# Expert picks of 64 tokens at a time: 64-column weight matrices in the two column halves of the array, in a one-core hybrid decoder step

## The chip, the core and the metric

One NeuronCore of one Trainium2 chip runs the whole program. The metric is device time in microseconds (us), as the median of several runs; durations inside the program come from one profiled execution. TensorE (PE in the profile) multiplies, VectorE (DVE), ScalarE (ACT) and GpSimd (POOL) do elementwise work, SyncE (SP) issues plain transfers, and sixteen DMA engines move data between HBM and SBUF. PEld in the profile is TensorE's weight load, which runs beside the multiplications.

## The reference

The program computes one step of a small decoder layer for 512 new tokens of one sequence and for 8 sample tokens of running sequences: two kinds of attention, an output projection, and then a layer of product-key experts ("PEER"). The change lies in the experts:

```
def peer(h, wq, subkeys, pu, pv):          # h: tokens x 1024
    q = (xb @ wq).reshape(blk, 8, 2, 128)
    s = einsum('thpc,hpnc->thpn', q, subkeys)          # 8 heads, 2 halves, 128 keys
    sv, si = top_k(s, 16)
    cand = sv[:, :, 0, :, None] + sv[:, :, 1, None, :]
    fv, fi = top_k(cand, 16)                            # 16 experts per token and head
    eidx = the expert numbers (of 16384);  gate = softmax(fv)
    act = gelu(einsum('thkd,td->thk', pu[eidx], xb)) * gate
    return einsum('thk,thkd->td', act, pv[eidx])
```

Each token has 8 heads of 16 picks. For each pick a row of `pu` (1024 floats) is multiplied with the token's row and summed, and a row of `pv` (1024 floats) is added to the token's result with the weight that comes of it. The two rows of an expert lie side by side in one table `peer_uv`, so a pick is one row of 8 KB. All data are float32.

## The kernel before

Before the experts come the projections, the attention and the page reads of the sample tokens; they take the first 870 us or so and none of that part is touched. The experts of the 512 prompt tokens are worked off in 4 tiles of 128 tokens, each of 8 heads, so in 32 units of 16 picks. A **step** is one pick of one head for all 128 tokens of a tile: there are 512 of them, and 8 more, one for each sample token with all its 128 picks, put in after unit 27. Steps are numbered g in the order in which they run.

For each step:

- `gather` on POOL issues one indirect DMA that brings 128 rows of 8 KB (1 MB), one for each partition, into one of `UN` = 8 buffers `UV` (six in the big ring `RING`, two in `R1` and `R2`). It first waits until `v_used` says that PE has finished step g - 8, the one before it in that buffer. On the same queue of POOL nothing else happens in this part.
- `dot` on DVE multiplies the first half of each row with the token's row `H2` and sums it (`SCALAR_TENSOR_TENSOR`, line 1797).
- `gelu` on ACT (line 1114) and `weigh` on DVE (line 1815) turn the sums of two steps into weights. They work on pairs of steps, so the second step of a pair holds back both.
- `diagonal` on ACT (line 1124) writes a matrix `DG` of 128 x 128: the identity, with each row scaled by its token's weight. There are 4 of them in turn.
- `value_step` on PE multiplies `DG` with the second half of the gathered rows, 512 columns at a time, and adds it in two PSUM banks (`lo`, `hi`) that a tile keeps for all its 128 steps:

```
pe.wait_ge(S(f"uv_in{g % UN}"), 16 * (g // UN + 1))
pe.wait_ge(S("diagonal"), k + 1)
mm(lo[:, :], DG[:, k % 4, :], UV[g % UN][:, 1024:1536], first, last)
mm(hi[:, :], DG[:, k % 4, :], UV[g % UN][:, 1536:2048], first, last, S("v_used"))
```

The order on every engine is written out by hand along **events** e: at event e POOL issues the gather of step e + 3, DVE takes the dot of step e, ACT at odd e the gelu of the steps e - 1 and e and the diagonals of e - 3 and e - 2, PE the value step of e - 4.

Between the steps of one tile the preparation of the next one is threaded in as **slots**, one at an event: 8 slots `wo` (`mix_part`: the output projection of the tile, two multiplications of 512 columns each; tile 3 has 16 of them, half of them for the 8 sample tokens), some for a norm and its transposes ("rest", "turn"), and 40 for queries and scores (`wq`, `score`). DVE works off the picks of the unit after next in pieces between its dots (`picks`), ACT the softmax of the gates (`gates`, with a table load before and one after it), DVE their scaling (`gate_scale`). At the start of each tile DVE takes the sums of the tile before out of PSUM, adds the residual, and normalises it. After the last step the last tile's sums go the same way. SP loads the weights of the slots (2 MB at a time), the tokens' rows and small vectors, and stores the results.

Of the kernel before, what the change touches and what calls it, by code (L numbers as in the profile page):

```python
# [8 lines left out]
ALU = mybir.AluOpType  # L9
# [3 lines left out]
P = 128  # L13
# [5 lines left out]
TILES = SEQ // P  # L19
# [13 lines left out]
def hybrid_decoder_step(nc, a, o):  # L33

    ctx = ExitStack()
    with ctx:
# [115 lines left out]
        G1S = part(R1, 7296, 1024)  # L152
        X1 = part(R1, 8320, 2048, n=2, d=D_MODEL)
# [7 lines left out]
        G2, G2S, FW = MV[:, 0, :], MV[:, 1, :], MV[:, 2, :]  # L161
# [26 lines left out]
        DG = part(R2, 11628, 512, n=4, c=P)  # L188
# [221 lines left out]
        def _(pe):  # L410
# [455 lines left out]
            def value_step(g, n, s_):  # L866
                t, h = divmod(n, PH)
                k = n * STEPS + s_
                lo, hi = banks[(t % 2) * 2], banks[(t % 2) * 2 + 1]
                first, last = h == 0 and s_ == 0, h == PH - 1 and s_ == STEPS - 1  # L870
# [17 lines left out]
            for e in events:  # L888
# [4 lines left out]
                elif n is not None:  # L893
                    value_step(g, n, s_)
# [10 lines left out]
        def _(act):  # L905
# [174 lines left out]

            def query_out(i, c, j):
# [34 lines left out]
            def diagonal(g):  # L1116
# [7 lines left out]
                A(DG[:, k % 4, :], ident[:, :], ACT.Copy, scale=AG[:, n % 4, s_:s_ + 1]).then_inc(S("diagonal"), 1)  # L1124

            for c in range(4):
                for j in range(4):
                    query_out(0, c, j)
                scores_out(0, c)
            gates(0)  # L1130

            def post_slot(i, kind, c=0, j=0, q=0):
# [6 lines left out]
                elif kind == "turn":  # L1139
                    second_turned(c, j)  # L1140
                elif kind == "wq" and q == 1:
# [27 lines left out]
        def _(dve):  # L1169
# [534 lines left out]
            step(V.tensor_copy(IOTA16, IOTAI))  # L1704
            job_done(dve, ("oT", 3, 1))
            settle()

            def picks(n, src, fv, eix):
# [50 lines left out]
                step(V.scalar_tensor_tensor(eix, R01[rows, 0, :], float(NKEY), R01[rows, 1, :], ALU.mult, ALU.add))  # L1759
# [27 lines left out]
            def dot(g):  # L1787
                n, s_ = steps_[g]
                if n % PH == s_ == 0 and n < UNITS:
                    dve.wait_ge(S("h_ready"), nth_h2(n // PH) + 1)  # L1790
# [5 lines left out]
                else:  # L1796
                    V.scalar_tensor_tensor(u, u, 1.0, H2[n // PH % 2], ALU.mult, ALU.mult, accum_out=DOT[:, n % 4, s_:s_ + 1]).then_inc(S("dots"), 1)  # L1797

            def gate_scale(n):
# [5 lines left out]
                step(V.tensor_scalar(GAT[:, x, :], GAT[:, x, :], SUMG[:, x:x + 1], None, ALU.mult))  # L1805
# [559 lines left out]
```

## Time and profile before

| | us |
|---|---|
| median of 3 runs | 2357.74 (2350.86 to 2362.78) |
| the profiled execution, as timed | 2358.1 |
| its span, first to last instruction | 2356.2 |

| engine | busy us | share of the span |
|---|---|---|
| PE | 1865.4 | 79% |
| DVE | 1372.6 | 58% |
| POOL | 873.8 | 37% |
| ACT | 508.2 | 22% |

What lies around the span is 1.9 us. Two things are to be kept in mind in reading it. A matmul of float32 data has two records in the profile, so a step's two multiplications of 512 columns appear as "x4", and a pair of steps as "x8". And a matmul's end is modelled: where records follow one another, the distance of their starts is what one costs. POOL's `DMA_INDIRECT` rows are the issue of a gather, not its transfer.

### The profile page before, as it was taken

Reading aid. Unit: us, or ns where it says so; the run is one execution under the profiler, and the core shown is the slowest. Engines: PE = TensorE matmul, PEld = TensorE weight load, DVE = VectorE, ACT = ScalarE, POOL = GpSimd, SP = SyncE. Lnnn points to the kernel's source line nnn. Section 1 sums busy time; section 2 is a strip of 40 time slices with the busy share of each in tenths; the row PEclk is TensorE's granted clock in tenths of the full one; section 3 lists DMA queues with packets and bytes.
Section 4 is the critical chain, followed back from the end, with each engine's and each line's share of the span. In section 5 each row is a group of like instructions: output and inputs, shape, how many; then the busy total and the mean of one; then the engine's idle time right before and its main releaser. Section 6 shows DMA issues by size and latency. Waiting matters only on the chain.

```text
span 2356.2 us, 24901 instructions
## 1 busy us (share of the span) xinstructions
PE 1865.4 (79%) x7984; PEld 1026.6 (44%) x7984; DVE 1372.6 (58%) x3247; ACT 508.2 (22%) x1333; POOL 873.8 (37%) x645
## 2 busy tenths in 40 slices
PE   2799977868988886788877789877798997776776
PEld 1455435557776773234532234532233552222222
DVE  3224755554555445666567666557666567764664
ACT  0101222211221122212212212222123222221221
POOL 0058563222322112433334443434333445433542
PEclk7788998879999988999999999999999999999999
DMA  7257740743432179999999999999999999999996
GB/s 264 72 195 240 246 165 12 250 134 119 144 124 94 60 259 416 420 410 405 416 411 412 399 389 415 415 415 403 412 381 353 403 396 407 387 421 418 378 420 283
DMA packets 168866, 728.26 MB, mean 309 GB/s; under 512 B 17757, under 2 KB 18750, under 8 KB 102034
## 3 DMA queue, kind: packets, MB, share of 16 engines
q0 software_dynamic: 75024, 545.82, 56.9%
q1 hardware_dynamic: 93714, 180.85, 22.2%
q8 instruction: 66, 1.08, 0.2%
q14 instruction: 62, 0.51, 0.1%
HBM read 720.66 MB, written 6.05 MB: 308 GB/s over the span
## 4 chain that ended last, share of the span: by engine, by line
PE 40%; DMA 33%; DVE 13%; issue 5%; POOL 4%; SPq 3%; ACT 2%; DVEq 0%; ACTq 0%; POOLq 0%
PE bank L412 38%; DMA RING<-in_peer_uv,R 20%; DMA R<-in_peer_uv,R 8%; DVE RING L1797 3%; SPq L2038 2%; PE bank L419 1%; DVE R L1797 1%; POOL MV L1945 1%; ACT R L1124 1%; DMA R<-h2s_d 1%; DMA MV<-in_cache_k 1%; DVE RING L1265 1%; DMA R<-in_x_sample 1%; DMA R<-in_x_prompt 1%; POOL RING L2024 1%
## 5 line engine op out<-in xcount | busy, mean ns | idle before, releaser
L412 PE MATMUL bank<-RING,R 128*128 128x512 f32 (+1 forms) x1560 | 756.7, 625 | 224.8 <-ACT R L1124 213.4
L2024 POOL DMA_INDIRECT RING<-in_peer_uv,R x390 | 444.7, 1140 | 738.4 <-PE bank L412 637.3
L412 PEld LDWEIGHTS bank<-RING,R 128*128 128x128 f32 (+1 forms) x1560 | 287.6, 196 | 625.2 <-issue 610.7
L412 PE MATMUL bank<-R 128*128 128x128 f32 (+5 forms) x2216 | 469.1, 365 | 87.6 <-ACT R L1124 71.8
L412 PEld LDWEIGHTS bank<-R 128*128 128x128 f32 (+3 forms) x2216 | 293.6, 192 | 253.0 <-issue 237.6
L1797 DVE SCALAR_TENSOR_TENSOR RING<-RING,R 128x1024 f32<-128x1024 f32 x192 | 234.9, 1225 | 171.7 <-DMA RING<-in_peer_uv,R 171.0
L1797 DVE SCALAR_TENSOR_TENSOR RING<-RING,MV 128x1024 f32<-128x1024 f32 x192 | 235.1, 1224 | 153.6 <-DMA RING<-in_peer_uv,R 152.6
L1114 ACT ACTIVATE R<-R 128x2 f32<-128x2 f32 x256 | 52.1, 203 | 1047.3 <-DVE RING L1797 840.6
L2024 POOL DMA_INDIRECT R<-in_peer_uv,R x130 | 151.3, 1164 | 208.8 <-PE bank L412 202.9
L1124 ACT ACTIVATE R<-ident,R 128x128 f32<-128x128 f32 x512 | 173.6, 386 | 0.4
L2002 POOL TENSOR_TENSOR R<-R,level 128x512 f32<-128x512 f32 x56 | 77.9, 1414 | 229.4 <-DVEq L1619 167.8
L1945 POOL TENSOR_TENSOR MV<-MV,RING 128x2048 f32<-128x2048 f32 x22 | 99.3, 4522 | 156.5 <-DMA RING<-samp_d 110.5
L412 PEld LDWEIGHTS bank<-HT,R 128*128 128x128 f32 x1024 | 134.0, 196 | 47.9 <-issue 46.8
L412 PE MATMUL bank<-HT,RING 128*128 128x512 f32 x320 | 142.0, 601 | 1.0 <-DVEq L1348 1.0
L412 PE MATMUL bank<-HT,R 128*128 128x128 f32 (+1 forms) x1024 | 135.0, 280 | 0.7 <-issue 0.7
L419 PE MATMUL bank<-ident,R 128*128 128x128 f32 (+2 forms) x310 | 59.3, 333 | 92.0 <-DVE R L1231 44.4
L1797 DVE SCALAR_TENSOR_TENSOR R<-R,MV 128x1024 f32<-128x1024 f32 x64 | 78.3, 1224 | 67.7 <-DMA R<-in_peer_uv,R 67.3
L1797 DVE SCALAR_TENSOR_TENSOR R<-R 128x1024 f32<-128x1024 f32 x64 | 78.3, 1223 | 67.1 <-DMA R<-in_peer_uv,R 66.9
L412 PE MATMUL bank<-RING,HT 128*8 128x128 f32 (+5 forms) x768 | 110.9, 361 | 4.6 <-ACT HT L1066 4.6
L1639 DVE TENSOR_TENSOR R<-R,bank 128x512 f32<-128x512 f32 x88 | 60.4, 688 | 65.8 <-PE bank L412 65.7
L412 PE MATMUL bank<-R,HT 128*128 128x64 f32 (+4 forms) x320 | 98.2, 439 | 0.0
L419 PEld LDWEIGHTS bank<-ident,R 128*128 128x128 f32 (+2 forms) x310 | 46.5, 180 | 109.5 <-DVE R L1231 48.5
(305 smaller groups left out, 1694.6 us busy)
## 6 DMA issues: line engine op xcount, KB each, us to landing
R<-in_peer_wq SPq DMA_DIRECT2D x16, 2048.0 KB, 25.0
RING<-in_w_mod SPq DMA_DIRECT2D x12, 2048.0 KB, 8.6
MV<-in_cache_k SPq DMA_DIRECT2D x88, 256.0 KB, 3.8
R<-in_cache_v SPq DMA_DIRECT2D x84, 256.0 KB, 3.8
R<-in_w_out SPq DMA_DIRECT2D x6, 2048.0 KB, 28.2
MV<-in_cache_v SPq DMA_DIRECT2D x44, 256.0 KB, 3.7
RING<-in_w_in SPq DMA_DIRECT2D x5, 2048.0 KB, 10.0
R<-in_cache_k SPq DMA_DIRECT2D x40, 256.0 KB, 3.9
```

The lines of the kernel that those rows point to most:

```text
L412: i = nc.tensor.matmul(out, lhsT, rhs, start=start, stop=stop, **k)
L419: i = nc.tensor.transpose(out, in_, ident[0:n, 0:n])
L1114: A(AG[:, n % 4, s_:s_ + 2], DOT[:, n % 4, s_:s_ + 2], ACT.Gelu).then_inc(S("gelu"), 1)
L1124: A(DG[:, k % 4, :], ident[:, :], ACT.Copy, scale=AG[:, n % 4, s_:s_ + 1]).then_inc(S("diagonal"), 1)
L1265: V.tensor_reduce(SC[:, :, n // 4, (n % 4) * 4:(n % 4) * 4 + 4].rearrange("p h g -> p g h"), pages(n).rearrange("p g (h d) -> p g h d", d= ...
L1639: V.tensor_tensor(dst, dst, b[:, :].rearrange("p (m c) -> p m c", m=4), ALU.subtract)\
L1797: V.scalar_tensor_tensor(u, u, 1.0, H2[n // PH % 2], ALU.mult, ALU.mult, accum_out=DOT[:, n % 4, s_:s_ + 1]).then_inc(S("dots"), 1)
L1945: T(k, k, QB[:, n // 4 % 2:n // 4 % 2 + 1, :].to_broadcast([P, 4, 512]), ALU.mult).then_inc(S("kprod"), 1)
L2002: T(M, AT, level[:, lv:lv + 1, :].to_broadcast([P, 4, P]), ALU.mult).then_inc(S(f"level{hb}"), 1)
L2024: nc.gpsimd.indirect_dma_start(UV[g % UN], None, a["peer_uv"][0], bass.IndirectOffsetOnAxis(ap=idx, axis=0)).then_inc(S(f"uv_in{g % UN}"), 16)
L2038: sp.dma_start(dst, src, **k).then_inc(S(sem), 16)
```

## The change

A gather now serves only 64 of a tile's 128 tokens and brings two of their picks. Of a pair of steps the even one belongs to the tokens 0 to 63 and the odd one to the tokens 64 to 127; in each, partitions 0 to 63 hold one pick and partitions 64 to 127 the next one of the same tokens. The number of gathers, their rows and their bytes stay, and so do the dots.

- The weight matrix of a step becomes 128 x 64: `FOLD`, two identities of 64 under one another, scaled by the rows' weights. It is computed once, by DVE, in a place that `hide_q` held.
- `value_pair` takes the place of two `value_step`: four multiplications, of which two write to partitions 0 to 63 of a bank and two to partitions 64 to 127. It waits for both gathers and both matrices, and adds to `v_used` once for each step, at the multiplications on `hi`.
- The dots of the odd steps need the rows of tokens 64 to 127 on all partitions, and those of the even steps the rows of tokens 0 to 63. `halves` on ACT makes them by three copies of 64 x 1024 for each tile, before the first tile's dots and then in the tile's second "turn" slot; DVE's first dot of a tile waits for them (`half_rows`) instead of for the norm.
- The numbers of the picks and the scaled gates are written in the new order: four operations on 64 x 8 each in place of one on 128 x 16 (in `picks` and in `gate_scale`).
- Places: `DG` and the scaled gates `GATS` go to free columns of `R1`, the new `H2HIGH` takes the places of `G2S` and `DG`, and `G2S` goes to where `G1S` was; its small load moves from before the steps to after the norm of the sample tokens.

```
-            def value_step(g, n, s_):
+            def value_pair(g, n, s_):
-                pe.wait_ge(S(f"uv_in{g % UN}"), 16 * (g // UN + 1))
-                pe.wait_ge(S("diagonal"), k + 1)
-                mm(lo[:, :], DG[:, k % 4, :], UV[g % UN][:, 1024:1536], first, last)
-                mm(hi[:, :], DG[:, k % 4, :], UV[g % UN][:, 1536:2048], first, last, S("v_used"))
+                for b in range(2):
+                    pe.wait_ge(S(f"uv_in{(g + b) % UN}"), 16 * ((g + b) // UN + 1))
+                pe.wait_ge(S("diagonal"), k + 2)
+                for bank, at in ((lo, 1024), (hi, 1536)):
+                    for b in range(2):
+                        mm(bank[64 * b:64 * b + 64, :], DG[:, (k + b) % 4, :], UV[(g + b) % UN][:, at:at + 512], first, last,
+                           S("v_used") if bank is hi else None)
...
-                    value_step(g, n, s_)
+                elif n is not None and g % 2 == 0:
+                    value_pair(g, n, s_)
...
+            def halves(t):
+                low, high = h2_rows(t)[0:64], h2_rows(t)[64:P]
+                act.wait_ge(S("h_ready"), nth_h2(t) + 1)
+                if t >= 2:
+                    act.wait_ge(S("dots"), at_step[(t - 1) * PH - 1, STEPS - 1] + 1)
+                A(H2HIGH[t % 2][64:P], high, ACT.Copy).then_inc(S("half_rows"), 1)
+                A(H2HIGH[t % 2][0:64], high, ACT.Copy).then_inc(S("half_rows"), 1)
+                act.wait_ge(S("half_rows"), 3 * t + 2)
+                job_done(act, ("h2T", t, 1))
+                A(high, low, ACT.Copy).then_inc(S("half_rows"), 1)
...
-                A(DG[:, k % 4, :], ident[:, :], ACT.Copy, scale=AG[:, n % 4, s_:s_ + 1]).then_inc(S("diagonal"), 1)
+                A(DG[:, k % 4, :], FOLD, ACT.Copy, scale=AG[:, n % 4, s_:s_ + 1]).then_inc(S("diagonal"), 1)
...
+                for a_, b in blocks:
+                    dst, src_ = slice(64 * a_, 64 * a_ + 64), slice(64 * b, 64 * b + 64)
+                    step(V.scalar_tensor_tensor(eix[dst, b:16:2], R01[src_, 0, a_:16:2], float(NKEY), R01[src_, 1, a_:16:2], ALU.mult, ALU.add))
...
-                    dve.wait_ge(S("h_ready"), nth_h2(n // PH) + 1)
+                    dve.wait_ge(S("half_rows"), 3 * (n // PH) + 3)
...
-                step(V.tensor_scalar(GAT[:, x, :], GAT[:, x, :], SUMG[:, x:x + 1], None, ALU.mult))
+                for a_, b in blocks:
+                    dst, src_ = slice(64 * a_, 64 * a_ + 64), slice(64 * b, 64 * b + 64)
+                    step(V.tensor_scalar(GATS[dst, x, b:16:2], GAT[src_, x, a_:16:2], SUMG[src_, x:x + 1], None, ALU.mult))
```

On PE, where the first `wo` slots of tile 1 stand among the value steps, before (`bank7` is the slot's, `bank0` and `bank1` are `lo` and `hi`):

```order
L412 MATMUL bank0<-RING,R2 128x512
L412 MATMUL bank1<-RING,R2 128x512
L412 MATMUL bank7<-R2,HT 128x512 x2
L412 MATMUL bank0<-RING,R2 128x512
L412 MATMUL bank1<-RING,R2 128x512
L412 MATMUL bank7<-R2,HT 128x512 x2
L412 MATMUL bank0<-R1,R2 128x512
L412 MATMUL bank1<-R1,R2 128x512
```

and the same place now:

```order
L416 MATMUL bank0<-RING,R1 64x512 x2
L416 MATMUL bank1<-RING,R1 64x512 x2
L416 MATMUL bank7<-R2,HT 128x512 x4
L416 MATMUL bank0<-R1 64x512
L416 MATMUL bank0<-R2,R1 64x512
L416 MATMUL bank1<-R1 64x512
L416 MATMUL bank1<-R2,R1 64x512
L416 MATMUL bank7<-R2,HT 128x512 x4
```

A pair of steps stands together, and the two slots that lay around its second step follow it as one block.

On ACT, at the second "turn" slot of tile 1, between the transposed rows' copy (`HT`) and the gates of the next unit, before:

```order
L1124 ACTIVATE R2<-ident,R2 128x128 x2
L1078 ACTIVATE HT<-bank6 128x4x128
L1106 ACT_TABLE_LOAD
L1106 ACTIVATE R2<-R2 128x16
L1114 ACT_TABLE_LOAD
L1114 ACTIVATE R2<-R2 128x2
```

and now:

```order
L1143 ACTIVATE R1<-hide_q,R2 128x64 x2
L1085 ACTIVATE HT<-bank6 128x4x128
L1094 ACTIVATE R2<-MV 64x1024
L1095 ACTIVATE R2<-MV 64x1024
L1098 ACTIVATE MV<-MV 64x1024
L1125 ACT_TABLE_LOAD
L1125 ACTIVATE R2<-R2 128x16
L1133 ACT_TABLE_LOAD
L1133 ACTIVATE R2<-R2 128x2
```

The three copies stand between the copy and the gates, ahead of the next gelu.

## Rows read from the trace of the kernel before

**Rows 1.** The page: busy time by engine, and GB/s in 40 slices of 58.9 us.
```profile
PE 1865.4 (79%) x7984; PEld 1026.6 (44%) x7984; DVE 1372.6 (58%) x3247; ACT 508.2 (22%) x1333; POOL 873.8 (37%) x645
GB/s 264 72 195 240 246 165 12 250 134 119 144 124 94 60 259 416 420 410 405 416 411 412 399 389 415 415 415 403 412 381 353 403 396 407 387 421 418 378 420 283
```

**Rows 2.** Waits, 900 to 2340 us: total, times, longest.
```profile
POOL RING L2024 <- PE bank L412: 637.3, 362, 17.6
```

**Rows 3.** Windows of 10 us: busy by engine, granted clock, DMA share, GB/s.
```profile
1040.00:1050.00 10.00, 10.00 (x25) 4.43 (x24) 8.04 (x21) 1.58 (x6) 3.59 (x4) 1.00 0.95 365
1700.00:1710.00 10.00, 7.40 (x17) 2.88 (x16) 5.68 (x13) 1.91 (x7) 4.19 (x4) 1.00 1.01 421
1750.00:1760.00 10.00, 10.00 (x23) 3.43 (x22) 5.11 (x14) 3.81 (x7) 3.45 (x3) 1.00 0.85 300
1920.00:1930.00 10.00, 10.00 (x48) 6.20 (x47) 6.58 (x16) 2.61 (x9) 4.25 (x5) 1.00 0.99 384
```

**Rows 4.** Timeline, steps without slots: start, duration, idle before and its releaser.
```profile
945.32 3.67 PE L412 MATMUL bank<-RING,R 128*128 128x512 f32 x8 [1.29 <-ACT R L1124]
947.55 0.94 POOL L2024 DMA_INDIRECT RING<-in_peer_uv,R  x1 [2.10 <-PE bank L412]
949.26 1.14 POOL L2024 DMA_INDIRECT RING<-in_peer_uv,R  x1 [0.78 <-PE bank L412]
950.27 3.67 PE L412 MATMUL bank<-RING,R 128*128 128x512 f32 x8 [1.28 <-ACT R L1124]
```

**Rows 5.** The chain of waits near the end: start, duration, what.
```profile
2329.08 8.98 DMA R<-in_peer_uv,R
```

**Rows 6.** Timeline of PE, `wo` slots of tile 3 among value steps.
```profile
1736.53 1.88 PE L412 MATMUL bank<-RING,R 128*128 128x512 f32 x4
1739.97 1.88 PE L412 MATMUL bank<-RING,R 128*128 128x512 f32 x4
1745.51 1.88 PE L412 MATMUL bank<-R,HT 128*8 128x512 f32 x4
1749.23 1.88 PE L412 MATMUL bank<-R,HT 128*8 128x512 f32 x4
```

**Rows 7.** Timeline of PE, earlier stages: multiplications in column groups.
```profile
446.87 1.04 PE L412 MATMUL bank<-R,RING 128*32 128x512 f32 x8
447.84 1.13 PE L412 MATMUL bank<-R,HT 128*128 128x512 f32 x2
800.03 1.09 PE L412 MATMUL bank<-R 128*64 128x128 f32 x16 [0.83 <-issue]
```

**Rows 8.** Timeline: PE after idle stretches, and a gather into an empty queue.
```profile
1271.67 3.67 PE L412 MATMUL bank<-R 128*128 128x512 f32 x8 [2.47 <-ACT R L1124]
1288.53 5.13 PE L412 MATMUL bank<-RING,R 128*128 128x512 f32 x8 [4.31 <-ACT R L1124]
...
1807.24 0.59 PE L419 MATMUL bank<-ident,R 8*128 8x8 f32 x4 [6.08 <-DVE R L1231]
1807.76 3.78 PE L412 MATMUL bank<-RING,R 128*128 128x512 f32 x4
...
1811.82 0.94 POOL L2024 DMA_INDIRECT RING<-in_peer_uv,R  x1 [9.45 <-PE bank L412]
1817.35 1.23 DVE L1797 SCALAR_TENSOR_TENSOR RING<-RING,R 128x1024 f32<-128x1024 f32 x1 [3.16 <-DMA RING<-in_peer_uv,R]
```

**Rows 9.** Timeline, the end (rows between left out).
```profile
2340.00 3.67 PE L412 MATMUL bank<-RING,R 128*128 128x512 f32 x8 [1.26 <-ACT R L1124]
...
2347.21 1.29 DVE L1822 TENSOR_TENSOR MV<-bank,MV 128x512 f32<-128x512 f32 x2 [7.46 <-PE bank L412]
```

**Rows 10.** Groups of instructions: busy us, mean ns, idle before.
```profile
L999 ACT ACTIVATE R<-R 128x1024 f32<-128x1024 f32 x4 | 4.2, 1048 | 0.0
L1106 ACT ACT_TABLE_LOAD x32 | 41.1, 1283 | 0.6
L1805 DVE TENSOR_SCALAR R<-R 128x16 f32<-128x16 f32 x32 | 7.5, 235 | 1.1
```

More of the change, by code:

```diff
@@ L152, in hybrid_decoder_step @@
         G1S = part(R1, 7296, 1024)
+        G2S = G1S
         X1 = part(R1, 8320, 2048, n=2, d=D_MODEL)
@@ L160, in hybrid_decoder_step @@
         UN = len(UV)
-        G2, G2S, FW = MV[:, 0, :], MV[:, 1, :], MV[:, 2, :]
+        G2, FW = MV[:, 0, :], MV[:, 2, :]
+        H2HIGH = [MV[:, 1, :], part(R2, 11628, 1024)]
+        FOLD = hide_q[:, 0:64]
         SX = part(R1, 10368, 256, p=2, n=P)
@@ L187, in hybrid_decoder_step @@
         NMX = R2[:, 11588:11592]
-        DG = part(R2, 11628, 512, n=4, c=P)
+        DG = part(R1, 11960, 256, n=4, c=64)
+        GATS = part(R1, 12216, 64, t=4, n=16)
         H2B = part(R2, 0, 2048, n=2, d=D_MODEL)
@@ L869, in value_step @@
                 lo, hi = banks[(t % 2) * 2], banks[(t % 2) * 2 + 1]
-                first, last = h == 0 and s_ == 0, h == PH - 1 and s_ == STEPS - 1
+                first, last = h == 0 and s_ == 0, h == PH - 1 and s_ == STEPS - 2
                 if first and t >= 2:
                     pe.wait_ge(S("sums_taken"), t - 1)
-                pe.wait_ge(S(f"uv_in{g % UN}"), 16 * (g // UN + 1))
-                pe.wait_ge(S("diagonal"), k + 1)
-                mm(lo[:, :], DG[:, k % 4, :], UV[g % UN][:, 1024:1536], first, last)
-                mm(hi[:, :], DG[:, k % 4, :], UV[g % UN][:, 1536:2048], first, last, S("v_used"))
+                for b in range(2):
[5 more added lines that the diff above has]
+                           S("v_used") if bank is hi else None)
             def sample_step(g, t):
@@ L1129, in _ @@
                 scores_out(0, c)
+                if c == 0:
+                    halves(0)
             gates(0)
@@ L1140, in post_slot @@
                     second_turned(c, j)
+                    if j == 1 and c < TILES:
+                        halves(c)
                 elif kind == "wq" and q == 1:
@@ L1704, in _ @@
             step(V.tensor_copy(IOTA16, IOTAI))
+            step(V.tensor_tensor(FOLD, ident[:, 0:64], ident[:, 64:P], ALU.add))
             job_done(dve, ("oT", 3, 1))
             settle()
+            blocks = [(a_, b) for a_ in range(2) for b in range(2)]
             def picks(n, src, fv, eix):
@@ L1758, in picks @@
                 settle()
-                step(V.scalar_tensor_tensor(eix, R01[rows, 0, :], float(NKEY), R01[rows, 1, :], ALU.mult, ALU.add))
+                if n < P:
+                    step(V.scalar_tensor_tensor(eix, R01[rows, 0, :], float(NKEY), R01[rows, 1, :], ALU.mult, ALU.add))
+                    return
+                for a_, b in blocks:
+                    dst, src_ = slice(64 * a_, 64 * a_ + 64), slice(64 * b, 64 * b + 64)
+                    step(V.scalar_tensor_tensor(eix[dst, b:16:2], R01[src_, 0, a_:16:2], float(NKEY), R01[src_, 1, a_:16:2], ALU.mult, ALU.add))
             def prompt_picks(n):
@@ L2277, in _ @@
             load(G2, mod_d[0:1, 5 * D_MODEL:6 * D_MODEL].to_broadcast([P, D_MODEL]), "g2_in")
-            load(G2S[0:NB], mod_d[1:9, 5 * D_MODEL:6 * D_MODEL], "g2_in")
             load(FW, a["final_norm_w"].rearrange("(o d) -> o d", o=1).to_broadcast([P, D_MODEL]), "g2_in")
@@ L2297, in post_slot @@
                     store(h2s_d, HS2[0:NB, :], "h2s_out")
+                    load(G2S[0:NB], mod_d[1:9, 5 * D_MODEL:6 * D_MODEL], "g2_in")
             def tile_out(t):
```

9 lines of the change are left out of this document (5 added, 4 removed).

## The prediction, made before the changed kernel had run

> **What bounds the kernel now.** I read the page first: PE is the busiest engine with 1865.4 us, but in the expert part, the last 24 whole slices before the end's, the DMA moves 353 to 421 GB/s [rows 1]. An average over such different stages decides nothing, so the second view is the waits of the expert part. There POOL has a long one, which wants to issue a gather and waits for PE to free a buffer, 637.3 us [rows 2]. That looks as if PE were the bound. The third view says otherwise: in a window without slots PE is busy 7.40 of 10 us and the DMA engines are full, share 1.01, 421 GB/s [rows 3]. At that rate a gather of 1.0486 MB takes 2.49 us, a pair 4.98, and a pair's two PE starts lie 4.95 apart [rows 4]. So without slots PE, ACT and DVE follow the DMA, and POOL's wait only says that the next gather is queued behind others that are still under way.
>
> How far it is queued is the number that decides this case. A gather that was issued after POOL had idled 9.45 us, with all others landed, was there 5.53 us later (the dot that waited for it starts at 1817.35, the issue is at 1811.82) [rows 8]. In steady running the second gather of a pair takes 8.98 us from issue to landing [rows 5]; the first is issued 1.71 us earlier [rows 4] and lands 2.49 earlier, so it takes 8.98 + 1.71 - 2.49 = 8.20. So the first gather of a pair is issued 8.20 - 5.53 = 2.7 us earlier than needed and the second 3.45 us. As long as a delay of PE is shorter than this, it costs nothing, and as long as there is such a margin, a faster PE brings nothing.
>
> PE is the bound only where the slots stand thick. A step costs it 1.72 us and a `wo` slot as much again: the value steps start 3.44 us apart, with the 8-row slots of tile 3 3.72 [rows 6], against 2.49 for the DMA. There PE is full for 10 of 10 us, and the rate falls to 365 in one window and 300 in the worst [rows 3]. I count thirteen windows of 10 us, the first and last of them in rows 3, in which PE was full or working off what had piled up, and the rate was below 400: 3 in tile 1, 2 in tile 2, 4 in tile 3, then 4 with its queries and scores. They moved 356.7 GB/s in the mean, so against 421 they lack 13 x 10 x (421 - 356.7) / 421 = 19.9 us.
>
> **The change part by part, against the profiled execution's 2358.1 us (its span of 2356.2 and 1.9 around it; the median of the runs is 0.4 below).**
>
> *Column halves.* Four multiplications of 32 columns in four column groups (8 records of 512) took 0.97 us from their first start to the next start of another shape, where one after the other they would take 8 x 0.43 = 3.44; 16 records of 64 columns and 128 long took 1.09, against 16 x 0.11 = 1.8 one after the other and their starts two at a time [rows 7]. 64 columns with 512 long do not occur, but lie between these. So I take a pair of steps as 1.72 us of PE, half of now. Where slots stand, PE changes its shape and back once for each pair; the 8-column slots show what that costs: 3.72 - 3.44 = 0.28 us [rows 6].
>
> *Where it counts.* In the `wo` stretches a pair with its two slots costs PE 6.87 now and 1.72 + 0.28 + 3.44 = 5.44 after, against 4.98 for the DMA. What is left, 0.46 us a pair, makes 1.9 us over the 4 pairs of tiles 1 and 2, within the margin, and 3.7 over the 8 of tile 3, which is 1.0 beyond it. A late start at a low clock (below) takes some more. Of the 19.9 us I take 15 as regained. All of them is the upper end. The lower end is the share that the DMA engines really stood still in these windows, from 0.85 to 1.02 against 1.01 without slots [rows 3]: 7.6 us over the thirteen.
>
> *The end.* The last four steps run on PE from 2340.00 to 2347.1, two pairs back to back, and DVE waits for them for 7.46 us [rows 9]. Nothing hides them. At the high clock the two pairs take 3.5 us instead of 7, at the low one 7. The first pair starts later, since it now waits for its second matrix too, by about 0.3. Between -3.2 and +0.3 us; I take -1.5.
>
> *The clock.* Without slots PE idles 1.29 us before each pair now [rows 4] and would idle 1.29 + 1.72 and the 0.3 less or more, some 3 us, with bursts of only 1.72. After an idle stretch of 2.47 us a pair took the 3.67 of the high level, after 4.31 it took 5.13, and after 6.08 one step took 3.78 where it takes 1.88 at the high one [rows 8], which is 1.2 GHz against 2.4. 3 us lies between, so I expect the granted clock to go back and forth in the stretches without slots. At the low level a pair in halves takes 3.44 us, what it takes now at the high one. The first gather of a pair, though, is freed only when all four are through: its margin is 2.7 - 0.3 - 1.72 = 0.7 us at the low clock and 2.4 at the high one. The second gather is issued 0.94 + 0.3 after the first, not 1.71 [rows 4]; its margin stays at 1.9 or more. So steady running still hides it, and only irregular places, at the start of a tile and around the sample steps, lose some: between 0 and 10 us for five such places, 4 taken.
>
> This is where a rule speaks against the change. The Trainium skill, TensorE: Matmul & The Clock Gate, section "HAM oscillation", says that bursts of matmuls shorter than the waits for DMA between them begin at half the clock each time. The rows bear it out at 4.31 and 6.08 us of idle time and don't show 3. By the rule the end gains nothing and the clock's term is at its upper end; that is the second rival.
>
> *ACT.* `halves` adds three copies; one of 128 x 1024 takes 1.05 us [rows 10], so some 3.2 us. In tile 3 and before the first tile other ACT work is far enough away. In tiles 1 and 2 they stand right ahead of the gates with their two table loads, 1.28 each [rows 10], in all some 6 us between a pair's matrices and the next gelu, where a pair's 4.98 us less some 1 for gelu and matrices are free. So it is late by 2 us twice, about what the margin holds: 0 to 4 us, 1 taken.
>
> *DVE.* In `gate_scale` four operations stand for one of 235 ns [rows 10], in `picks` four for one like it. That adds at most 6 x 0.235 = 1.4 us a unit, 45 in all, to an engine that idles 2 to 5 of 10 us [rows 3]. Where it is behind already, at the tiles' starts, it costs something: 0 to 4 us, 1 taken. Ahead of the first gather three of them stand on the path, 0.5 us. The matrix `FOLD` is one operation, the moved load of `G2S` is 32 KB and waited for only by the sample tokens, and `half_rows` is reached long before a tile's first dot: nothing.
>
> *Sum:* -15 - 1.5 + 4 + 1 + 1 + 0.5 = -10. 2358.1 - 10 = **2348 us**. The bounds give 2358.1 - 19.9 - 3.2 = 2335 and 2358.1 - 7.6 + 0.3 + 10 + 4 + 4 + 0.5 = 2369.
>
> **The rivals.** *More is regained.* If the rest of what the rate lacks comes back as well, since PE works off a pile twice as fast: where DVE or the clock had made it. The 24 slices of 58.9 us average 404.3 GB/s, so they lack 24 x 58.9 x (421 - 404.3) / 421 = 56 us against 421 [rows 1], 20 of them in the thirteen windows. All of the 20, the end and 8 of the other 36 give 2358 - 20 - 3 - 8 + 2 = 2329. For it: the terms against me are only estimates. Against it: most of the 36 lie in windows where the DMA engines had no idle time, and a faster PE gives them nothing.
>
> *The clock eats it.* The `wo` slots begin at the low level, where one costs 3.44 us instead of 1.72, and PE is behind before the clock rises. Then 7.6 regained, nothing at the end, 6 lost at irregular places, 2 for ACT and DVE: 2358.5, no change. Also without effect would be halves that don't run side by side (a pair at 3.44 us as now); rows 7 speak plainly against that.
>
> *Slower: the margin of 0.7 us runs out.* At the low clock the first gather of a pair is issued 0.7 us before the DMA would run dry. If the path from a landing through dot, gelu, weights and two matrices to PE gets longer by more than 0.7 us in ordinary running, each pair without slots (about 340 steps, 170 pairs) at the low clock loses what is beyond. With 0.25 us beyond on 100 pairs that is 25 us, and 2358.1 - 10 + 25 = 2373. For it: PE's idle time will be long in all these stretches, and DVE's pieces of picks, now longer, stand in that path. Against it: the dot usually starts at the landing, and POOL's two issues follow closer.
>
> **How the numbers follow.** 0.5% is 12 us, about what a measurement of this kernel can tell from no change; so faster is below 2346. The forecast, with 2340 to 2356 around it, has 0.6, and four tenths of that lie below 2346. More regained 0.18, the clock or no overlap 0.11, slower 0.11. Faster: 0.24 + 0.18 = 0.42. Slower by 12 us: 0.1 of the 0.11. The rest, 0.48, is within. The range for 8 in 10 is 2331 to 2367: it leaves out the far ends of the first and the last rival.
>
> **What would show it.** In the profile after: a pair as 16 half-width records of which two start together, 1.72 to 1.9 us at the high clock; windows without slots with the same 421 GB/s and PE at 3.5 to 7 of 10 us; a lower mean granted clock; the windows of the `wo` slots at over 400 GB/s; DVE's last wait for PE at 4 to 7 us. I am wrong if the rate without slots falls below 415, if pairs take 3.4 us at the high clock, or if the rate in the `wo` slots stays where it was.

## The result, and the profile after

The changed kernel takes 2412.5 us (median of 4 runs, 2404.3 to 2421.2) against 2354.3 us for the kernel before in the same session (4 runs, 2346.8 to 2362.8): a ratio of 1.025, 95% interval 1.019 to 1.031. It is slower by 58 us; I had forecast 10 us faster and given slower 0.10. Its profiled execution took 2419.0 us, its span is 2417.2.

The page after, with the granted clock and the rate in slices of 60.4 us, answers to [rows 1]; the line of the waits, 900 to 2400 us (total, times, longest), to [rows 2]:

```profile
PE 1636.8 (68%) x7984; PEld 827.0 (34%) x7984; DVE 1415.0 (59%) x3440; ACT 492.0 (20%) x1345; POOL 872.0 (36%) x645
...
PEclk6798988879999886789876778977796886767777
...
GB/s 266 62 206 223 257 141 49 239 126 85 158 141 53 187 285 383 389 394 412 410 398 373 373 381 415 415 390 374 383 402 322 404 405 362 385 380 383 389 361 284
```
```profile
POOL RING L2059 <- PE bank L416: 626.9, 189, 19.4
```

PE is busy for 229 us less, and the rate falls to 373 to 390 GB/s in slices without slots. POOL waits as long as before, but in half as many pieces: two buffers now come free together. Windows of 10 us (busy by engine, granted clock, DMA share, GB/s): the first three without slots, the fourth in tile 1's `wo` slots, the last two in tile 3's slots. They answer to [rows 3].

```profile
940.00:950.00 10.00, 5.62 (x16) 1.42 (x16) 5.25 (x17) 4.33 (x10) 5.29 (x6) 0.73 0.95 362
...
960.00:970.00 10.00, 4.77 (x12) 1.18 (x12) 5.35 (x13) 1.36 (x6) 4.84 (x5) 0.67 0.98 372
970.00:980.00 10.00, 6.56 (x16) 1.37 (x12) 7.16 (x18) 0.68 (x3) 2.62 (x3) 0.70 0.96 368
...
1040.00:1050.00 10.00, 9.72 (x26) 3.29 (x27) 7.75 (x24) 1.50 (x7) 4.21 (x4) 0.83 0.98 353
```
```profile
1780.00:1790.00 10.00, 10.00 (x30) 2.45 (x30) 7.46 (x21) 4.33 (x10) 3.74 (x4) 1.00 0.99 386
1790.00:1800.00 10.00, 10.00 (x30) 3.07 (x28) 8.08 (x26) 1.36 (x6) 4.92 (x4) 1.00 1.01 408
```

Where nothing but the pairs runs, 421 GB/s have become 362 to 372, which is the first of my signs of being wrong (below 415). No engine that computes is busy for over 7.2 of 10 us. The DMA engines' share is still 0.95 to 0.98, so they move fewer bytes in their busy time. A window of `e8_before_later_129` below, with the old rows and matrices, has 0.93 at 357 GB/s: this goes with late gathers, and not with the new rows. The timeline of that stretch (start, duration, idle before and its releaser), rows of PE, POOL and DVE, answers to [rows 4]:

```profile
956.24 1.71 POOL L2059 DMA_INDIRECT RING<-in_peer_uv,R  x1 [5.44 <-PE bank L416]
...
962.55 3.54 PE L416 MATMUL bank<-RING,R 128*64 128x512 f32 x8 [1.79 <-ACT R L1143]
...
964.49 1.22 DVE L1828 SCALAR_TENSOR_TENSOR RING<-RING,R 128x1024 f32<-128x1024 f32 x1 [2.46 <-DMA RING<-in_peer_uv,R]
...
966.85 0.94 POOL L2059 DMA_INDIRECT RING<-in_peer_uv,R  x1 [3.11 <-PE bank L416]
...
968.09 1.38 POOL L2059 DMA_INDIRECT RING<-in_peer_uv,R  x1 [0.30 <-issue]
```
```profile
980.83 1.94 PE L416 MATMUL bank<-R 128*64 128x512 f32 x8 [1.36 <-ACT R L1143]
```

The halves do run side by side: 1.94 us a pair at the high clock, 3.54 at the low one. But at the low one POOL issues the first gather of the next pair at 966.85, 4.3 us after PE's start at 962.55, and in the chain below 3.8 us after it (979.67 after 975.90); before it was 2.23 us (947.55 after 945.32 [rows 4]). The chain of waits (start, duration, what) goes round exactly there, from PE by way of POOL's issue and a gather to the dot, the matrices and PE again; it answers to [rows 5]:

```profile
962.80 10.98 DMA R<-in_peer_uv,R
973.80 1.25 DVE R L1828 x2
975.09 0.07 issue
975.18 0.58 ACT R L1143 x2
975.76 0.14 issue
975.90 3.58 PE bank L416 x8
979.48 0.19 issue
979.67 1.11 POOL RING L2059
980.77 0.31 issue
981.08 8.26 DMA RING<-in_peer_uv,R
```

Where the 62 us went shows in the time between the last landings of the gathers, summed over stretches. This table, and the one on leads further below, are worked out from the issue and landing times of the 520 gathers of each trace (us; in the last column's trace 65 landings are missing, none of them at the border of a stretch). The kernels of the other columns are told of in the next section: "filled behind" is `e1_idle_filled`, "single steps" `e2_single_steps`, "short before" `e3_before_short`, "short path" `e4_short_path` (with the halves) and `e5_short_before` (with 128 columns), "filled ahead" `e6_filled_ahead`, and "before+" the kernel before with its buffers freed 0.86 or 1.29 us later. The traces of the four runs from `e9_before_wait_both` on have no landings:

```
stretch                 steps before after  filled single short  short path  filled  before+ before+
                                            behind steps  before halves/128  ahead   0.86    1.29
without slots (5)        328   864.5 926.8  886.6  907.6  853.1  851.6/849.5  956.5   884.0   912.7
wo slots (3)              41   130.5 122.6  120.1  137.9  120.2  116.6/116.8  124.4   129.2   129.6
query, score slots (3)   126   379.7 389.6  385.2  378.6  384.2  383.5/382.7  386.7   377.6   376.2
```

The `wo` stretches gave back 7.9 us. The stretches without slots lost 62.3, and they had been written down as safe. The query and score stretches, which the prediction had gaining a part of its 15 us, lost 9.9; 7.8 of that lie in tile 3, and the experiment on the stall comes back to it.

### The profile page after: what moved, and what is told of

It reads as the page before. It is cut to its first block, busy times and chain, and to the rows that moved or that the text cites. A ratio compares the mean times of both kernels' runs of the same rounds, so it can differ in the third digit from the quotient of the medians.

```text
span 2417.2 us, 24891 instructions
## 1 busy us (share of the span) xinstructions
PE 1636.8 (68%) x7984; PEld 827.0 (34%) x7984; DVE 1415.0 (59%) x3440; ACT 492.0 (20%) x1345; POOL 872.0 (36%) x645
## 4 chain that ended last, share of the span: by engine, by line
DMA 39%; PE 28%; DVE 13%; POOL 8%; issue 7%; ACT 3%; SPq 3%; DVEq 0%; ACTq 0%; POOLq 0%
PE bank L416 26%; DMA RING<-in_peer_uv,R 23%; DMA R<-in_peer_uv,R 10%; DVE RING L1828 3%; POOL RING L2059 3%; POOL MV L1980 2%; SPq L2073 2%; ACT R L1143 2%; PE bank L423 1%; DVE R L1828 1%; DMA R<-h2s_d 1%; POOL R L2059 1%; POOL R L1980 1%; DMA R<-mod_d 1%; DMA R<-in_x_sample 1%
## 5 line engine op out<-in xcount | busy, mean ns | idle before, releaser
L416 PE MATMUL bank<-RING,R 128*64 128x512 f32 (+1 forms) x1560 | 552.5, 832 | 423.0 <-ACT R L1143 411.2
L416 PE MATMUL bank<-R 128*128 128x128 f32 (+5 forms) x2216 | 406.8, 418 | 172.1 <-ACT R L1143 156.2
L416 PEld LDWEIGHTS bank<-RING,R 128*64 128x64 f32 (+1 forms) x1560 | 137.9, 171 | 785.5 <-issue 769.4
L416 PEld LDWEIGHTS bank<-R 128*128 128x128 f32 (+3 forms) x2216 | 244.9, 188 | 333.5 <-issue 318.8
L2059 POOL DMA_INDIRECT R<-in_peer_uv,R x130 | 145.7, 1121 | 235.9 <-PE bank L416 215.2
L1143 ACT ACTIVATE R<-hide_q,R 128x64 f32<-128x64 f32 x512 | 146.3, 332 | 0.3 <-issue 0.2
L416 PEld LDWEIGHTS bank<-HT,R 128*128 128x128 f32 x1024 | 127.4, 202 | 49.9 <-issue 48.8
L1288 DVE TENSOR_REDUCE RING<-MV 128x32 f32<-128x2048 f32 x22 | 50.2, 2285 | 63.2 <-POOL MV L1980 63.1
```

What stands on the lines that cost most here:

```text
L416: i = nc.tensor.matmul(out, lhsT, rhs, start=start, stop=stop, **k)
L1143: A(DG[:, k % 4, :], FOLD, ACT.Copy, scale=AG[:, n % 4, s_:s_ + 1]).then_inc(S("diagonal"), 1)
L1288: V.tensor_reduce(SC[:, :, n // 4, (n % 4) * 4:(n % 4) * 4 + 4].rearrange("p h g -> p g h"), pages(n).rearrange("p g (h d) -> p g h d", d= ...
L2059: nc.gpsimd.indirect_dma_start(UV[g % UN], None, a["peer_uv"][0], bass.IndirectOffsetOnAxis(ap=idx, axis=0)).then_inc(S(f"uv_in{g % UN}"), 16)
```

## The experiments

Theory A: what counts is when the first buffer of a pair comes free; the low clock moves that moment, and there is next to no margin. Rivals: the pairing alone, whatever the clock (B); slower transfers of the new rows (C); a single stall.

**Work behind each pair, to keep the clock up** (`e1_idle_filled`).

```
+            def idle_work(e, n):
+                ...
+                for x in range(2):
+                    for b in range(2):
+                        mm(banks[((t + 1) % 2) * 2 + x % 2][64 * b:64 * b + 64, :], FOLD, other, True, True)
...
                     value_pair(g, n, s_)
+                    idle_work(e, n)
```

> The changed kernel, with four more multiplications of 512 columns (constants, into the banks of the other tile, whose content is thrown away) behind each pair of steps where no slot stands. PE works longer, and nothing else is changed. Theory A (the low clock makes a pair 3.5 us instead of 1.9, and since both of its buffers come free only at its end, the first gather is issued too late): the granted clock goes back to 0.9 or more, pairs take 1.7 to 1.9 us, the windows without slots move over 410 GB/s, and 50 of the 62 us go: 2350 to 2366. Theory B (the pairing of the two steps alone, whatever the clock): clock up, time 2400 to 2420. Theory C (the gathers themselves move more slowly since they bring other rows): also 2400 to 2420, with the DMA engines' share at 1.0 and the rate at 370 to 390 GB/s.

The edit leaves out the first 16 steps of each tile, so 137 pairs have the added work.

Measured: 2362.1 us, ratio 1.004 (1.002 to 1.006), mean clock 0.893. With more work on PE, 50 us of the 58 are gone. Its windows show the clock rise and the rate with it:

```profile
930.00:940.00 10.00, 3.94 (x13) 1.02 (x12) 5.97 (x17) 1.36 (x6) 4.91 (x4) 0.70 0.99 388
940.00:950.00 10.00, 9.01 (x32) 2.70 (x28) 6.74 (x21) 4.33 (x10) 4.06 (x4) 0.78 0.99 399
950.00:960.00 10.00, 7.33 (x34) 2.58 (x34) 8.00 (x24) 1.36 (x6) 3.79 (x5) 1.00 1.01 416
960.00:970.00 10.00, 7.39 (x34) 2.60 (x36) 7.61 (x21) 1.36 (x6) 4.35 (x4) 1.00 1.01 421
```

The same gathers reach 421 GB/s, so C falls, and B can be no more than the rest, 9 us and the 10 that the `wo` stretches gained (120.1 against 130.5).

**The same work ahead of each pair** (`e6_filled_ahead`): the four multiplications stand between the waits and the pair.

> The changed kernel with the four multiplications on constants ahead of each pair without slots, instead of behind it: PE's work and so the clock are as there, but both buffers of a pair are freed 1.7 us later, as late as at the low clock. Theory A (only the time of release counts, with a margin of some 0.4 us before the first gather is too late): 2395 to 2415 at a mean clock of 0.88 or more. If the low clock costs in another way (it slows a path that the release has no part in): 2355 to 2370, as with the work behind the pair.

Measured: 2448.5 us, ratio 1.039 (1.036 to 1.043), mean clock 0.873. The same work at nearly the same clock, moved from behind the pair to ahead of it, costs 86 us. So the time of release alone makes such losses, at a high clock too. The size is above my range: 86 us for 1.7 us of delay, some 50 us for each microsecond. A window without slots:

```profile
960.00:970.00 10.00, 5.60 (x26) 1.78 (x22) 5.34 (x16) 0.68 (x3) 4.20 (x5) 1.00 0.97 355
```

**The kernel before, with short multiplications** (`e3_before_short`).

```
-                mm(lo[:, :], DG[:, k % 4, :], UV[g % UN][:, 1024:1536], first, last)
-                mm(hi[:, :], DG[:, k % 4, :], UV[g % UN][:, 1536:2048], first, last, S("v_used"))
+                mm(lo[:, 0:256], DG[:, k % 4, :], UV[g % UN][:, 1024:1280], first, last)
+                mm(hi[:, 0:256], DG[:, k % 4, :], UV[g % UN][:, 1536:1792], first, last, S("v_used"))
```

> The kernel before, with each value multiplication on only 256 of its 512 columns, so half of the experts' output is left out. A pair of steps costs PE 1.72 us at the high clock as in the changed kernel, but each step still frees its buffer by itself, and the gathers bring the old rows. Theory A (low clock and release of both buffers at the end together): the mean clock falls to 0.80 to 0.85, yet the rate without slots stays near 420 GB/s: 2335 to 2355. If the low clock alone is enough: 2390 to 2415. Theory C (slower transfers of the new rows): 2335 to 2355, too, so it is told apart by the one with single steps.

Measured: 2335.3 us, ratio 0.992 (0.989 to 0.996), mean clock 0.828, at the lower end of the range that A and C share. The stretches without slots take 853.1 us where the kernel before has 864.5: a low clock by itself costs nothing there, if the first release of a pair is early. At 3.46 us for a pair at the low clock the first step is through after half of it:

```profile
967.46 3.46 PE L412 MATMUL bank<-RING,R 128*128 128x256 f32 x8 [2.36 <-ACT R L1124]
```
```profile
950.00:960.00 10.00, 7.07 (x20) 4.50 (x18) 7.14 (x22) 1.58 (x6) 4.52 (x5) 0.66 1.01 422
```

**Column halves, but each step on its own** (`e2_single_steps`).

```
...
+                pe.wait_ge(S(f"uv_in{g % UN}"), 16 * (g // UN + 1))
+                pe.wait_ge(S("diagonal"), k + 1)
+                mm(lo[64 * b:64 * b + 64, :], DG[:, k % 4, :], UV[g % UN][:, 1024:1536], first, last)
+                mm(hi[64 * b:64 * b + 64, :], DG[:, k % 4, :], UV[g % UN][:, 1536:2048], first, last, S("v_used"))
```

> The changed kernel with the matrices of 64 columns, but each step multiplied on its own when its own matrix is there, and its buffer released at its own end. Theory B (pairing alone): all of it comes back, 2345 to 2360. Theory A (low clock and pairing together): the first buffer of a pair comes free after half of the pair's work, so most comes back even with a mean clock of 0.8 to 0.85: 2355 to 2380, and a gather rate of over 405 GB/s where no slots stand. Theory C (slower transfers): stays at 2400 to 2420.

Measured: 2409.4 us, ratio 1.024 (1.020 to 1.028), mean clock 0.841. The expectations of A and B missed. The time lies in C's range, but with the same rows the windows of `e1_idle_filled` reach 421 GB/s, so it is no evidence for C. I had thought that a step on its own frees its buffer after half of the pair's time. It doesn't: the two steps of a pair, issued one after the other, still overlap, and each takes about as long as both do together. In this kernel's trace a pair takes 3.80 us at the low clock and 2.14 at the high one, and POOL gets its buffer only at the end of it:

```profile
962.15 3.80 PE L416 MATMUL bank<-RING,R 128*64 128x512 f32 x8 [2.81 <-ACT R L1141]
967.45 2.14 PE L416 MATMUL bank<-RING,R 128*64 128x512 f32 x8 [1.49 <-ACT R L1141]
```
```profile
965.91 1.71 POOL L2057 DMA_INDIRECT RING<-in_peer_uv,R  x1 [3.58 <-PE bank L416]
```

So the delay is in the half-width multiplications themselves, and undoing the pairing in the program's order doesn't give it back. In the `wo` stretches it is even worse (137.9 us), since a step between slots finds no partner to overlap with. There one step alone takes from 1043.36 to 1045.22, 1.86 us, as much as a whole pair and more than the 1.72 of a step of 128 columns [rows 6]:

```profile
1043.36 1.93 PE L416 MATMUL bank<-R 128*64 128x512 f32 x4
1045.22 1.98 PE L416 MATMUL bank<-R,HT 128*128 128x512 f32 x4
```

**The kernel before, released later at the high clock** (`e7_before_later_086`, `e8_before_later_129`): constants are multiplied ahead of 137 pairs without slots. The edit of the first is shown; the second adds a multiplication of 256 columns behind it.

```
+                if h and s_ % 2 == 0 and not slots_of(g + BEHIND) and not slots_of(g + BEHIND + 1):
+                    ...
+                    mm(banks[((t + 1) % 2) * 2][:, 0:512], ident[:, :], level[:, 0:4, :].rearrange("p l c -> p (l c)")[:, 0:512], True, True)
```

> The kernel before with one multiplication of 128 x 512 on constants ahead of each pair of steps without slots (some 140 pairs): both steps free their buffers 0.86 us later, at the high clock, and PE is busy for 4.3 of a pair's 4.98 us. It measures the margin by itself. With the 2.7 us of my prediction nothing happens: 2348 to 2360. Theory A: traces show that the interval between landings grows once the first gather of a pair is issued less than some 5.3 us before the landing of the one ahead, and steady running has 5.7, a margin of 0.4; what lies beyond it goes round the ring of four pairs once, so a pair loses a quarter of it: 140 x (0.86 - 0.4) / 4 = 16 us, 2362 to 2378.

> As the one with 0.86 us, with 256 columns more, so each buffer is freed 1.29 us later; PE is busy for 4.73 of a pair's 4.98 us. With a margin of 2.7 us nothing happens: 2348 to 2362. Theory A, margin 0.4: 140 x (1.29 - 0.4) / 4 = 31 us, 2375 to 2395.

Measured: 2379.1 us, ratio 1.013 (1.009 to 1.016), and 2406.2 us, ratio 1.023 (1.020 to 1.026). This is the prediction's margin, measured on the kernel before with nothing of the change in it. A margin of 2.7 us is refuted. So is the size that theory A gave here, 16 and 31 us where 30 and 53 were lost. The same sum with no margin at all gives 137 x 0.86 / 4 = 29 and 137 x 1.29 / 4 = 44: it fits the first and is somewhat low for the second, and it was made afterwards. Windows of the second of the two, at the full clock:

```profile
950.00:960.00 10.00, 9.40 (x24) 4.21 (x23) 6.19 (x20) 1.81 (x7) 4.37 (x4) 1.00 0.97 377
...
970.00:980.00 10.00, 8.88 (x22) 3.83 (x22) 7.19 (x20) 1.58 (x6) 4.44 (x5) 1.00 0.93 357
```

**The kernel before, waiting for both matrices** (`e9_before_wait_both`).

```
+                if s_ % 2 == 0:
+                    pe.wait_ge(S(f"uv_in{(g + 1) % UN}"), 16 * ((g + 1) // UN + 1))
+                    pe.wait_ge(S("diagonal"), k + 2)
```

> The kernel before, in which PE waits for both matrices and both gathers of a pair before the first of its two steps, as the changed kernel does; nothing else is changed. The first buffer of each pair is freed some 0.35 us later, the second as before. With work behind the pairs, which keeps the clock up, the changed kernel was still 9 us above the kernel before, though its stretches with wo slots were 12 us faster. If the wait for the second matrix is that rest: 2362 to 2375. If the margin of 0.4 to 0.6 us, which the runs with a later release show, holds it back: 2351 to 2360.

Measured: 2378.9 us against 2359.7 for the kernel before in its session, ratio 1.008 (1.005 to 1.010). That is above both ranges as they stand; counted as a difference it is the loss that the first of them expected, and a margin of 0.4 to 0.6 us doesn't hold it back. The second matrix is one more of these (groups: mean ns; of the kernel before, then of the one after):

```profile
L1124 ACT ACTIVATE R<-ident,R 128x128 f32<-128x128 f32 x512 | 173.6, 386 | 0.4
```
```profile
L1143 ACT ACTIVATE R<-hide_q,R 128x64 f32<-128x64 f32 x512 | 146.3, 332 | 0.3 <-issue 0.2
...
L1838 DVE TENSOR_SCALAR R<-R 64x8 f32<-64x8 f32 x128 | 30.4, 237 | 4.2
L1790 DVE SCALAR_TENSOR_TENSOR R<-R 64x8 uint32<-64x8 f32 x128 | 20.8, 163 | 4.1
```

0.39 us of delay costs 18 us (11 to 24). With 0.86 for 30 and 1.29 for 53 that is 35 to 46 us for each microsecond. The three aren't quite alike: here only the first buffer of a pair comes free later, but in all 256 pairs, there both do, in 137. Even so none shows a first part that is free: on the average over a tile there is no margin that can be seen.

**The kernel before, with the change's DVE work** (`e12_before_more_dve`): four operations for one in `picks` and in `gate_scale`, in the old order.

> The kernel before, with only the changed kernel's additional DVE work: the numbers of the picks and the scaled gates written by four operations of 64 x 8 each in place of one of 128 x 16, in the old order. If this is the rest of what the changed kernel loses with its clock up: 2362 to 2375. With my prediction's term (1 us taken, 4 the bound): 2352 to 2358.

Measured: 2364.6 us, ratio 1.0035 (1.0015 to 1.0055), so 4 to 13 us. The time lies at the lower end of the first range, but its session's kernel before was at 2359.7, some 6 us higher than in the sessions from which the ranges came; the difference, 8 us, lies between the two expectations, and above the term of the prediction.

**A shorter path from landing to release** (`e4_short_path` on the changed kernel, `e5_short_before` on the one before).

```
-        AHEAD, BEHIND = 3, 4
+        AHEAD, BEHIND = 3, 2
...
-                    for g in (e - 3, e - 2):
+                    for g in (e - 1, e):
                         if 0 <= g < len(steps_):
                             diagonal(g)
...
-                if e % 2 == 0 and 0 <= e // 2 - 1 < len(steps_) // 2:
-                    weigh(e // 2 - 1)
...
+                if e % 2 and e // 2 < len(steps_) // 2:
+                    weigh(e // 2)
```

> The changed kernel with a shorter path from a landing to the release of its buffer: the weights of a pair are taken on DVE in the odd event itself, the matrices on ACT in the same event right behind the gelu, and PE multiplies the pair two events earlier in its order. The low clock stays as it is. Theory A (the release comes too late by a part of a microsecond to two): the gathers are issued earlier, the rate without slots rises over 410 GB/s at a mean clock still near 0.8, and 2340 to 2365. Theory C (slower transfers): 2400 to 2420. A theory in which the clock alone slows something else than the release: 2400 to 2420 too.

> The kernel before, 128-column matrices, with the same shorter path from landing to release as in the changed one above (weights of a pair in the odd event, matrices right behind the gelu, PE's step two events earlier). It says how much of the gain over the kernel before comes from the shorter path, and how much from the column halves. Theory A: without slots the kernel before loses some 8 us that a longer lead gives back, the slots stay bound by PE, 13 to 17 us of the changed one's gain stay away: 2338 to 2350, so 0.993 to 0.998 of before. If the shorter path did it all: 2325 to 2332, the same as the changed kernel with it.

Measured: 2328.7 us, ratio 0.989 (0.985 to 0.993), and 2327.1 us, ratio 0.989 (0.986 to 0.991). Both beat both kernels of this case, and they are equal. The first is faster than theory A's range, the second in the range of "the shorter path did it all". With the column halves the clock is still low, 0.823 in the mean, and it does no harm:

```profile
930.00:940.00 10.00, 6.87 (x20) 1.79 (x18) 7.23 (x20) 1.58 (x6) 2.96 (x3) 0.54 1.01 421
940.00:950.00 10.00, 4.93 (x18) 1.43 (x16) 6.78 (x22) 4.54 (x10) 5.66 (x6) 0.84 1.01 422
```
```profile
2270.87 14.03 DMA RING<-in_peer_uv,R
```

A gather now has 14.03 us from issue to landing near the end, where the kernel before had 8.98 [rows 5]. With 128 columns the same path makes up for what PE lacks in the `wo` slots of tile 1, 420 GB/s with PE full where it was 365 [rows 3]; in tile 3 the worst window stays:

```profile
1040.00:1050.00 10.00, 10.00 (x25) 4.42 (x24) 7.58 (x21) 1.79 (x6) 3.36 (x3) 1.00 1.01 420
```
```profile
1740.00:1750.00 10.00, 10.00 (x22) 2.97 (x22) 3.78 (x8) 3.97 (x7) 1.88 (x2) 1.00 0.90 305
```

So the whole gain is the shorter path's, and my expectation that the column halves would keep 13 to 17 us of it was wrong. Which of its three edits does it was not tried apart.

**The stall in tile 3** (`e10_short_before_gap`, `e11_short_halves_gap`). In the changed kernel DVE waits once for a small load that lies behind weights on SP's queue (waits, 1820 to 1850 us):

```profile
DVE small L1250 <- DMA R<-mod_d: 11.1, 1, 11.1
```

The edit puts four empty slots ahead of it: `slots += [("rest", 6)] * 4 + [("rest", 3), ("turn", 4, 0), ("turn", 4, 1)]`.

> The kernel before with the shorter path, and four empty slots in tile 3 ahead of the norm of the sample tokens. There DVE waits for the load of two small rows that lies behind 4 MB of weights on SP's queue (1.0 us in the kernel before, 11.1 in the changed one, 10.0 in it with the shorter path), and all dots wait with it. With 4 events more, some 10 us, the load should be there. If that stall costs what the gap in the landings shows (8 us): 2317 to 2322. If the DMA engines only catch up on the weights in that time: 2325 to 2329, as without the empty slots.

> The changed kernel with the shorter path and the same four empty slots. It says whether the column halves are worth anything once the lead is long and the stall is gone. If they are not: the same as the kernel before with both, within 3 us. If PE is what holds the slots: 4 to 8 us below it.

Measured: 2326.4 us, ratio 0.986 (0.983 to 0.989), and 2330.4 us, ratio 0.987 (0.984 to 0.990). Both traces no longer show that wait, and both times are what they were without the empty slots, within the intervals; the second is 4.0 us above the first where I had allowed 3. With the shorter path the stall costs nothing that can be measured, and the column halves are still worth nothing. The changed kernel itself, without the shorter path, was not run this way. There the stall may well cost something: between two gathers' landings in that place lie 12.7 us (4.9 in the kernel before), the query stretch of tile 3 is 7.8 us longer than before, and 4.7 longer in `e1_idle_filled`, whose wait is 9.5 us, while `e2_single_steps` with a wait of 0.3 is 2.0 shorter. This is outside the 62 us of the stretches without slots.

## Why the prediction was wrong

*The step that failed* is the margin. I wrote that the first gather of a pair is issued "2.7 us earlier than needed", and took from it that steady running hides the low clock. What is needed came from a gather into an empty queue, 5.53 us from issue to dot [rows 8], of which 2.49 are its own transfer: so it could be issued 3.04 us before the landing ahead of it. Under load that isn't enough. Here are the 163 first gathers of pairs without slots, sorted by lead, the time from their issue to the landing of the gather ahead (number, and the mean interval between the two landings, us; 2.49 is the full rate):

```
lead us      before       after        filled behind  before + 0.86  halves, short path
under 4      3   4.38     25   3.78    14   3.91      13   3.68        2   3.24
4 to 5      12   3.05     33   3.44    14   3.42      53   2.87        3   3.03
5 to 5.5    19   2.72     24   2.75    23   2.68      21   2.69        2   2.83
5.5 to 6.5  98   2.55     34   2.63    69   2.59      55   2.59        3   2.91
over 6.5    31   2.76     47   2.66    43   2.66      21   2.75      153   2.55
```

Below a lead of 5 us, and not only below 3, the interval is clearly longer; from 5 to 5.5 it is about what it is above 6.5. In the kernel before the median lead is 5.8, and 34 of the 163 are already below 5.5. After the change 58 of them are below 5, which by this table cost 25 x (3.78 - 2.6) + 33 x (3.44 - 2.6) = 57 us over the 2.6 of the others; before 15 of them cost 3 x 1.8 + 12 x 0.45 = 11. That makes 46 of the 62 us that these stretches lost. The table sorts and doesn't prove: the lead isn't all that counts, since in the row from 4 to 5 the interval is 3.4 in both kernels that free two buffers at once and 2.9 to 3.1 in the two columns of the kernel before (the short path has only 3 gathers there). That a late release is the cause is shown by the runs with a moved release. My sum of 8.20 - 5.53 compared a time under load with one without. The Trainium skill, DMA: Bandwidth & Descriptors, section "Latency and other measured facts", gives the access to HBM as 0.2 us in the mean and 2 us at high load, and calls it the larger part of a transfer's fixed cost. The 2 us between a lead of 3.0 and one of 5 are of that size, but no run here separates this latency from uneven engines.

*A second error beside it:* I took one steady place [rows 4] for all 328 steps. A margin is also what lets a ring of buffers catch up behind the picks' pieces and the gates. With none, each small delay stays; this would be how 0.39 us cost 18, and it is argued, not tried.

*The terms.* Column halves, 1.72 us a pair and 0.28 for the change of shape: right (at the low clock 3.54 where I had 3.44). In tile 3's slots a pair and two slots take 1.87 and 3.53 us,

```profile
1799.77 1.94 PE L416 MATMUL bank<-R 128*64 128x512 f32 x8
1801.64 3.60 PE L416 MATMUL bank<-R,HT 128*8 128x512 f32 x8
1805.17 1.94 PE L416 MATMUL bank<-RING,R 128*64 128x512 f32 x8
```

so 5.40 where I had 5.44; it answers to [rows 6]. The Trainium skill, TensorEngine Tiling (Array Packing), section "Key Properties", says that a change of the tiling mode drains the engine; these rows give the price, 5.40 - 1.72 - 3.44 = 0.24 us for both changes of a pair. *The 15 us regained* were 7.9. Four of my thirteen windows lay in the query slots, whose stretches take 376 to 390 us in every kernel of the table, the changed one at the upper end: there the DMA engines' share was 0.99 at 384 GB/s already [rows 3], and a faster PE gives nothing. That the 2 MB weight loads are what fills them was not tried. *The end:* the first of the two last pairs begins at 2402.64 at the low clock, the second 3.44 later, and DVE waits 5.98 us instead of 7.46 [rows 9]:

```profile
2402.64 3.68 PE L416 MATMUL bank<-RING,R 128*64 128x512 f32 x8 [1.31 <-ACT R L1143]
...
2406.08 1.98 PE L416 MATMUL bank<-R 128*64 128x512 f32 x8
...
2408.20 1.29 DVE L1856 TENSOR_TENSOR MV<-bank,MV 128x512 f32<-128x512 f32 x2 [5.98 <-PE bank L416]
```

From the last landing to the end it is 16.7 us instead of 18.1: -1.4, as forecast. *The clock's place* was foreseen, its price was not: 4 us taken, 10 the bound, 50 measured (2412.5 against 2362.1 with the clock kept up). At some 45 us for each microsecond that would be a first release later by 1.1 us in the mean (an estimate), out of the 1.72 that the low clock adds. The rule that the prediction cites (the Trainium skill, TensorE: Matmul & The Clock Gate, "HAM oscillation") agrees with the windows after, where the granted clock is 0.67 to 0.73 in the mean. What half the clock costs is another matter: 50 us in the changed kernel, nothing in the kernels with the short path. *The second matrix*, folded into the margin at 0.3 us, is 18 us (11 to 24). *DVE*, 1 taken and 4 the bound, is 4 to 13 on the kernel before. Together -7.9 - 1.4 + 50 + 18 + 8 = 67 against 58 measured, within the intervals of the parts, which need not add up. ACT's three copies, 1.05 us each as foreseen, and the stall in tile 3 of the changed kernel, at which the prediction had no term, were not tried alone.

The rival "the margin of 0.7 us runs out" named the place and the mechanism, and priced it at 25 us with a chance of 0.11. The trace of the kernel before could have warned: its 15 gathers with a lead below 5 us already landed late (3.05 and 4.38 us after the one ahead, in the means of the two rows).

## What to carry to other kernels

How early a transfer must be issued is read under load: sort the trace's transfers by their lead and find where the interval between landings begins to grow. An empty queue's latency says too little. An engine that is not the bound still sets when buffers come free, so making its work denser while each piece takes as long, or starts later, can cost more than its idle time suggests. A shorter path from landing to release is worth more here than a faster multiplication (26 us, on the kernel before, where the halves on top of it gave none), and with it neither the clock nor the faster multiplication makes a difference that can be measured.

## What was not expected of the hardware

A first gather needed a lead of about 5 us at 421 GB/s, where 3.0 would do into an empty queue. Single 64-column steps in opposite halves overlap into 2.14 us at the high clock and 3.80 at the low one with no pairing in the program. And more work on an engine made a program 50 us faster: with four multiplications on constants behind 137 pairs the mean granted clock was 0.89 instead of 0.81.
